# One projection stage of a hybrid decoder: the sample tile with its upper and lower parts side by side as one stationary operand

## What is computed

```python
def ab_project(x, pos, w_in):
    bn, n_len, _ = x.shape
    qa, ka, va, qb, kb, vb, gb = jnp.split(x @ w_in, 7, axis=-1)
    heads = lambda t: t.reshape(bn, n_len, -1, HEAD_DIM)
    return (rope(heads(qa), pos), rope(heads(ka), pos), heads(va),
            rope(heads(qb), pos), rope(heads(kb), pos), heads(vb), gb)
```

## Time and profile before

| | us |
|---|---|
| median of 3 runs | 2499.44 |
| lowest and highest | 2494.7, 2500.23 |
| span of the profiled execution | 2499.5 |
| PE busy | 2399.3 (96%) |
| DVE busy | 1621.7 (65%) |
| ACT busy | 1082.6 (43%) |
| all 28 pieces of PB1 and PB2, from first product to last | about 57 and 73 |

### The profile page before, as it was taken

One profiled execution on the slowest core, in us unless ns is written; L12 is line 12 of the kernel. 1 busy time (PEld: TensorE's weight loads), 2 busy tenths in 40 slices (PEclk: granted clock), 3 DMA queues, 4 the chain that ended last, 5 costly groups with the idle time before them and its releaser, 6 DMA issues.

```text
span 2499.5 us, 46319 instructions
## 1 busy us (share of the span) xinstructions
PE 2399.3 (96%) x18807; PEld 2262.1 (91%) x18807; DVE 1621.7 (65%) x2539; ACT 1082.6 (43%) x1657; POOL 468.4 (19%) x535
## 2 busy tenths in 40 slices
PE   7989999999899999999999999999999999999998
PEld 7988998999788777788999999999999898999997
DVE  5787776666775555577686566466656585587555
ACT  3433355433554333353353534455433637354332
POOL 4886810001200021300111101021001010121001
PEclk9999999999999999999999999999999999999998
DMA  8657766435446687644666556555554566555553
GB/s 181 172 161 206 206 186 202 127 110 152 118 143 200 194 281 219 176 121 110 172 175 174 164 152 198 182 154 155 152 152 144 174 196 204 151 168 144 153 151 105
DMA packets 676421, 417.84 MB, mean 167 GB/s; under 512 B 31570, under 2 KB 639698, under 8 KB 676210
## 3 DMA queue, kind: packets, MB, share of 16 engines
q1 hardware_dynamic: 669682, 394.51, 54.8%
q0 software_dynamic: 6528, 20.37, 2.6%
HBM read 396.04 MB, written 18.78 MB: 166 GB/s over the span
## 4 chain that ended last, share of the span: by engine, by line
PE 76%; DVE 13%; ACT 4%; issue 3%; SPq 2%; DMA 2%; POOL 1%; DVEq 0%; ACTq 0%; POOLq 0%
PE ps L270 21%; PE ps L272 20%; PE ps L271 20%; DVE w_lo L265 4%; PE ps L1004 2%; PE ps L1005 2%; PE ps L1006 2%; ACT w_hi L256 2%; PE ps L2403 1%; PE ps L1716 1%; PE ps L1765 1%; DMA w_raw<-in_ffn_w_up 1%; PE ps L1737 1%; DVE h_lo L467 1%; DVE x L557 1%
## 5 line engine op out<-in xcount | busy, mean ns | idle before, releaser
L265 DVE TENSOR_TENSOR w_lo<-w_raw,w_hi 128x1024 fp32r<-128x1024 f32 (+1 forms) x648 | 824.6, 1277 | 615.6 <-ACT w_hi L256 612.8
L270 PE MATMUL ps<-x_hi,w_hi 128*128 128x256 f32 (+1 forms) x3200 | 970.6, 303 | 33.6 <-DVE w_lo L265 23.7
L271 PE MATMUL ps<-x_lo,w_hi 128*128 128x256 f32 (+1 forms) x3200 | 955.3, 299 | 0.0
L272 PE MATMUL ps<-x_hi,w_lo 128*128 128x256 f32 (+1 forms) x3200 | 955.1, 298 | 0.0
L256 ACT ACTIVATE w_hi<-w_raw 128x1024 fp32r<-128x1024 f32 (+1 forms) x648 | 670.3, 1035 | 583.4 <-PE ps L272 419.6
L270 PEld LDWEIGHTS ps<-x_hi,w_hi 128*128 128x128 f32 x3200 | 615.5, 192 | 53.4 <-DVE w_lo L265 37.2
L271 PEld LDWEIGHTS ps<-x_lo,w_hi 128*128 128x128 f32 x3200 | 615.8, 192 | 1.1 <-issue 0.2
L272 PEld LDWEIGHTS ps<-x_hi,w_lo 128*128 128x128 f32 x3200 | 615.5, 192 | 0.0
L270 PE MATMUL ps<-h_hi,w_hi 128*128 128x256 f32 (+1 forms) x1408 | 422.5, 300 | 12.9 <-DVE w_lo L265 9.4
L271 PE MATMUL ps<-h_lo,w_hi 128*128 128x256 f32 (+1 forms) x1408 | 414.2, 294 | 0.0
L272 PE MATMUL ps<-h_hi,w_lo 128*128 128x256 f32 (+1 forms) x1408 | 414.2, 294 | 0.0
(11 more groups left out here) (281 smaller groups left out, 2184.5 us busy)
## 6 DMA issues: line engine op xcount, KB each, us to landing
w_raw<-in_ffn_w_gate SPq DMA_DIRECT2D x176, 512.0 KB, 4.1
w_raw<-in_ffn_w_up SPq DMA_DIRECT2D x176, 512.0 KB, 3.9
w_raw<-in_ffn_w_down SPq DMA_DIRECT2D x128, 512.0 KB, 4.0
w_raw<-in_w_in_ab SPq DMA_DIRECT2D x56, 512.0 KB, 4.1
w_raw<-in_ffn_w_down SPq DMA_DIRECT2D x64, 384.0 KB, 3.6
arena<-in_cache_k SPq DMA_DIRECT2D x64, 256.0 KB, 4.3
arena<-in_cache_v POOLq DMA_DIRECT2D x64, 256.0 KB, 4.7
w_raw<-in_w_out_ab SPq DMA_DIRECT2D x16, 512.0 KB, 4.0
```

The source lines that it names most:

```text
L265: dve.tensor_tensor(T.w_lo[:, u % RING, 0:n], T.w_raw[:, u % RAW, 0:n], T.w_hi[:, u % RING, 0:n].bitcast(F32), ALU.subtract).then_inc(T.w_ ...
L270: pe.matmul(out, w_hi, m_hi, start=first, stop=False)
L271: pe.matmul(out, w_hi, m_lo, start=False, stop=False)
L272: return pe.matmul(out, w_lo, m_hi, start=False, stop=last)
```

## The change

For the samples' tile alone, the 64 upper parts and the 64 lower parts are laid side by side as one stationary operand of 128 columns (`sample_tokens`, in the place of `h_hi`, which is free then). One product with `w_hi` gives hi·hi on partitions 0 to 63 and lo·hi on 64 to 127; a second, with the 64 upper columns alone and `w_lo`, adds hi·lo to partitions 0 to 63. So there are two products for each block instead of three. At the end of every section ACT moves partitions 0 to 63 to partitions 64 to 127 of a buffer in SBUF (`sample_rests`, in the place of `prod`), DVE adds that to the bank, and only then ACT empties it. At the start of PB1 and of PB2 ACT copies the samples' upper and lower parts into place, when PE has used all earlier pieces. The rotation of the samples' tile works on 64 partitions instead of 128.

Elsewhere, three counters (`h_rounded`, `rs_zeroed`, `zeroed`) become uses of the chain counter of DVE; at one place two memsets are then waited for one by one.

```diff
@@ class Project
+        self.rests = T.rests_moved.take(len(sections) if PT in self.tiles else 0)
+        self.copied = T.samples_copied.take(2 if PT in self.tiles else 0)
+        T.rests_added.close(len(sections) if PT in self.tiles else 0)
...
+def sample_tokens(T):
+
+    return T.h_hi.rearrange("p f n -> p (f n)")[:, 0:KT * P].rearrange("p (k n) -> p k n", k=KT)
+
+
+def sample_rests(T):
+
+
+    return T.prod[NS:P, :, :].rearrange("p a n -> p (a n)")[:, 0:MIX]
@@ project_tensor
+                if t == PT:
+                    if kk == 0:
+                        pe.wait_ge(T.samples_copied.h, R.copied + 2)
+                    both, own = sample_tokens(T)[:, kk], sample_tokens(T)[:, kk, 0:NS]
+                    if kk == 0:
+                        pe.matmul(out, both, w_hi, start=True, stop=False, skip_group_check=True)
+                        mm = pe.matmul(out[0:NS], own, w_lo, start=False, stop=False, skip_group_check=True)
+                    else:
+                        pe.matmul(out[0:NS], own, w_lo, start=False, stop=False, skip_group_check=True)
+                        mm = pe.matmul(out, both, w_hi, start=False, stop=(kk == KT - 1), skip_group_check=True)
+                    continue
                 pe.matmul(out, x_hi, w_hi, start=(kk == 0), stop=False)
                 pe.matmul(out, x_hi, w_lo, start=False, stop=False)
                 mm = pe.matmul(out, x_lo, w_hi, start=False, stop=(kk == KT - 1))
@@ project_scalar
-            act.activation(dst, T.ps[:, T.banks[R.o + n * j + i], 0:MIX], ACT.Silu if s == G_B else ACT.Copy)\
-               .then_inc(T.staged.h, 1)
+            out, r = T.ps[:, T.banks[R.o + n * j + i], 0:MIX], slice(NS if t == PT else 0, P)
+            if t == PT:
+                act.activation(sample_rests(T), out[0:NS], ACT.Copy).then_inc(T.rests_moved.h, 1)
+                act.wait_ge(T.rests_added.h, R.rests + j + 1)
+            act.activation(dst[r], out[r], ACT.Silu if s == G_B else ACT.Copy).then_inc(T.staged.h, 1)
...
     for sem, value in R.clear:
         act.wait_ge(sem.h, value)
+    if PT in R.tiles:
+        act.wait_ge(T.w_used.h, R.u)
+        if R.x_ready is not None:
+            act.wait_ge(T.x_ready.h, R.x_ready + KT)
+        for i, src in enumerate((T.x_hi, T.x_lo)):
+            act.activation(sample_tokens(T)[:, :, i * NS:(i + 1) * NS], src[:, :, SEQ:NT], ACT.Copy)\
+               .then_inc(T.samples_copied.h, 1)
@@ project_vector (rotate: every operand on partitions `at`, NS to P for the samples' tile)
+        at = slice(NS if t == PT else 0, P)
...
+        if q == 3 and PT in R.tiles:
+            out = T.ps[NS:P, T.banks[R.o + n * j + n - 1], 0:MIX]
+            dve.wait_ge(T.rests_moved.h, R.rests + j + 1)
+            dve.tensor_tensor(out, out, sample_rests(T), ALU.add).then_inc(T.rests_added.h, 1)
         yield
@@ S5Prepare, vector
-                    dve.memset(self.kernel[n][0:GH, :, 0:P], 0.0).then_inc(S.zeroed.h, 1)
-                dve.wait_ge(S.zeroed.h, 2)
+                    T.dve_chain(dve, dve.memset(self.kernel[n][0:GH, :, 0:P], 0.0))
```

More of the change, by code:

```diff
@@ L196, in open_trunk @@
     T.y_moved = [count("y_moved0"), count("y_moved1")]
-    T.tanh_done, T.silu_done, T.glu_done, T.h_rounded, T.h_done = map(
-        count, ("tanh_done", "silu_done", "glu_done", "h_rounded", "h_done"))
+    T.tanh_done, T.silu_done, T.glu_done, T.h_done = map(
+        count, ("tanh_done", "silu_done", "glu_done", "h_done"))
     T.res_done, T.acc_added, T.sum_done, T.centred = map(count, ("res_done", "acc_added", "sum_done", "centred"))
@@ L205, in open_trunk @@
     T.halves_added, T.scaled = count("halves_added"), count("scaled")
+    T.samples_copied, T.rests_moved, T.rests_added = map(count, ("samples_copied", "rests_moved", "rests_added"))
     T.dve_chain = Chain(ctx, nc, "dve_chain")
@@ L369, in __init__ @@
         self.u, self.o = len(T.pieces), len(T.banks)
-        self.tanh, self.silu, self.glu, self.rounded, self.h = (
-            c.take(n) for c in (T.tanh_done, T.silu_done, T.glu_done, T.h_rounded, T.h_done))
+        self.tanh, self.silu, self.glu, self.h = (
+            c.take(n) for c in (T.tanh_done, T.silu_done, T.glu_done, T.h_done))
         self.res_before = None if part == 0 else F.res
@@ L1057, in rotate @@
         t, r = R.tiles[i], n * R.nth[s] + i
+        at = slice(NS if t == PT else 0, P)
+        m = at.stop - at.start
         dve.wait_ge(T.staged.h, R.staged + n * j + i + 1)
[L1059 to L1063, removed]
+        heads = M.stage[at, i].rearrange("p (h j d) -> p h j d", h=HEADS, j=2)
+        sums = by_sin[at].rearrange("p (h j d) -> p h j d", h=HEADS, j=2)
+        dve.tensor_tensor(by_cos[at].rearrange("p (h d) -> p h d", d=HD // 2),
+                          M.stage[at, i].rearrange("p (h d) -> p h d", d=HD // 2),
+                          M.cos[at, t:t + 1, :].to_broadcast([m, HEADS * 2, HD // 2]), ALU.mult)
         for k in range(2):
             last = dve.tensor_tensor(sums[:, :, k], heads[:, :, 1 - k],
-                                     M.sin[:, t, k:k + 1, :].to_broadcast([P, HEADS, HD // 2]), ALU.mult)
+                                     M.sin[at, t, k:k + 1, :].to_broadcast([m, HEADS, HD // 2]), ALU.mult)
         T.dve_chain(dve, last)
-        dst = M.kb[R.g][:, i] if s == K_B else M.rot[:, i]
+        dst = M.kb[R.g][at, i] if s == K_B else M.rot[at, i]
         if s != K_B and R.turned + r >= n:
@@ L1072, in rotate @@
             dve.wait_ge(T.k_stored.h, M.k_stored[R.g])
-        last = dve.tensor_tensor(dst, by_cos, by_sin, ALU.add)
+        last = dve.tensor_tensor(dst, by_cos[at], by_sin[at], ALU.add)
         if s in (Q_B, K_B):
             T.dve_chain(dve, last)
-            d = (M.dq if s == Q_B else M.dk)[:, t, :].unsqueeze(2).to_broadcast([P, HEADS, HD])
+            d = (M.dq if s == Q_B else M.dk)[at, t, :].unsqueeze(2).to_broadcast([m, HEADS, HD])
             last = dve.tensor_tensor(dst.rearrange("p (h d) -> p h d", h=HEADS),
@@ L1546, in pick @@
                .then_inc(T.rs_picked.h, 1)
-        dve.memset(self.q_of[:, :, :, :], 0.0).then_inc(T.rs_zeroed.h, 1)
-        dve.wait_ge(T.rs_zeroed.h, 1)
+        T.dve_chain(dve, dve.memset(self.q_of[:, :, :, :], 0.0))
         for b in range(DEC_BATCH):
@@ L1994, in open_s5 @@
     S.made_taps = nc.dram_tensor("s5_made_taps", (KT, P, GT * P), F32, kind="Internal").ap()
-    S.sized, S.fallen, S.inverted, S.b_loaded, S.c_loaded, S.c_turned, S.c_placed, S.zeroed = map(
-        count, ("sized", "fallen", "inverted", "b_loaded", "c_loaded", "c_turned", "c_placed", "zeroed"))
+    S.sized, S.fallen, S.inverted, S.b_loaded, S.c_loaded, S.c_turned, S.c_placed = map(
+        count, ("sized", "fallen", "inverted", "b_loaded", "c_loaded", "c_turned", "c_placed"))
     S.formed, S.b_turned, S.b_moved, S.c_done, S.tapped, S.placed = map(
```

7 lines of the change are left out of this document (3 added, 4 removed).

## The result

The changed kernel takes 2511.31 us (2511.03 to 2511.73 over four runs) against 2499.14 before: a ratio of 1.005, 95% interval 1.0037 to 1.0063. It is slower, as forecast, by almost twice the forecast's 6.5 us, and 0.3 us above the range's upper end.

What follows compares the result with a forecast made beforehand. PE and DVE were taken as level in PB1 and PB2, so saved products become waits. Step-by-step delays of +2.3 us and clock drops of 4.4 gave +6.7 on 2499.44: 2506 us, range 2497 to 2511.

Steps and rivals of the forecast that it cites:

- What bounds the stages: In PB1 and PB2 PE and DVE are level; at four turns PE can come no earlier, however few its products.
- The rival in which PE's gain shows: Move and addition find engines free, nothing hangs on DVE, so 12.7 − 0.9 us goes: 2488 us; chance 0.08.
- Move and addition: At each section's end, 0.68 + 0.76 = 1.44 us between PE's last product and ACT's third emptying.
- step (c): In PB1, K_A's reciprocal waits for move and addition; the turn comes at 695.3 instead of 694.72, after waiting 3.4 us.
- The clock: Half-clock drops behind new waits of 3.4, 3.5 and 5.2 us in PB1 and PB2, 1.7 us each: together 4.4 us.
- step (a): At PB1's start the samples' first product waits for the copies, 1.3 us later; ACT's move comes at 662.1.
- the walk: Step-by-step timing without clock drops: PB1's third emptying 2.1 us later, PB2's end 0.15 later, +2.3 us in all.
- the rival without drops: The new waits in PB1 and PB2 leave the clock up, so only +2.3 us: 2501.8 us; chance 0.32.
- Drains: Changes between 64 and 128 columns drain PE, adding 1.6 us in PB1, 1.7 in PB2: 2509.5 with drops; chance 0.15.
- The change does what it says: Check against a rival that it does not: PE's list is 14934 rows instead of 14990, 56 fewer.
- What would show it: Turn waits of about 2, 3.4, 3.5, 5.2 us; K_A's reciprocal behind the addition; FFN's gate near 709 to 710.

Runs made afterwards that it cites:

- e2: The changed kernel without ACT's move and DVE's addition, the upper half of the samples' products left out of the result: 2498.61 us, ratio 0.9997.
- e10: The changed kernel with copies awaited one piece later, the addition one step later and writing the third emptying's output, unused products before four turns: 2495.47 us, ratio 0.9986.
- e5: The changed kernel with unused products into an unused bank, ahead of the waits at the four turns and before PB1's first samples' product: 2503.16 us, ratio 1.0013.
- e8: The changed kernel with DVE's addition one step later, writing straight to the third emptying's place except in G_B: 2499.25 us, ratio 0.9995.
- e12: The changed kernel itself, run again beside later experiments: 2511.70 us, ratio 1.005.
- e1: The changed kernel with unused products before each samples' turn, into the bank the turn will write, behind the wait for ACT: 2510.54 us, ratio 1.004.
- e3: The change in PB1 alone, PB2 multiplying as in the kernel before: 2505.47 us, ratio 1.0025.
- e6: The changed kernel with three products per part in the samples' first piece and the copies awaited one piece later: 2507.35 us, ratio 1.003.
- e7: The changed kernel with DVE's addition one step later, behind the norm's step that stood behind it: 2509.55 us, ratio 1.0037.

## Why the sign was right and the size was not

**What bounds the stages** was right. PE's saved products became waits at the turns, at all four; e2 shows that they are worth nothing that can be measured even when the sum is free, because of the waits and of the drops behind them. Only where fillings take those drops away, too (e10), do 3.1 us of the 12.7 show. The rival in which PE's gain shows is out for the change as made.

**Move and addition** were right in size. The timeline of ACT in the changed kernel, at the end of Q_A:

```profile
663.10 0.59 ACT L1054 ACTIVATE prod<-ps 64x512 f32<-64x512 f32 x1 [0.33 <-PE ps L1027]
664.47 0.60 ACT L1056 ACTIVATE arena<-ps 64x512 f32<-64x512 f32 x1 [0.78 <-DVE ps L1129]
```

And the timeline of DVE, the additions of Q_A and K_A, the reciprocal behind the second:

```profile
663.72 0.71 DVE L1129 TENSOR_TENSOR ps<-ps,prod 64x512 f32<-64x512 f32 x1 [1.90 <-ACT prod L1054]
...
683.83 0.71 DVE L1129 TENSOR_TENSOR ps<-ps,prod 64x512 f32<-64x512 f32 x1 [3.06 <-ACT prod L1054]
684.57 1.75 DVE L553 RECIPROCAL rstd<-rstd 128x256 f32<-128x256 f32 x1
```

Move to third emptying is 664.47 − 663.10 = 1.37 us (1.44 was taken), the addition 0.71 (0.69). The reciprocal stands behind the addition as step (c) said: K_A's move starts 5.9 us behind the first turn, and the turn follows the move by 15.1, where (c) had 4.2 and 15.0; the 1.7 us between 5.9 and 4.2 is, but for 0.1 to 0.2, the stretch at half clock from 677.7 to 681.0.

**The clock** is the step that failed, as the sum's term "together 4.4". It was worked out from three waits, those over 3.3 us, with one short drop at each. There were six behind this change in the trace, five of them at the copies and the turns, and three of those ran 5 us or more. The wait at the copies was in step (a) as 1.3 us of delay, which was right (the samples' first product is 6.82 from the start instead of 5.42), but not as a wait that lowers the clock; the first turn's 1.9 us was held too short for it, on the evidence of one wait of 2.50 without a drop, beside one of 2.20 with a drop. In numbers, at 47% of each stretch that lies on PE's products: PB1 6.1, 3.3 and 6.5 us (647.6 to 653.7, 677.7 to 681.0, 698.4 to 704.9) cost 2.9 + 1.5 + 3.1 = 7.5. With the walk's 2.1 that is 9.6; the third emptying is 66.21 − 56.75 = 9.5 later. PB2: 3.4 and 5.0 us cost 1.6 + 2.35, with 0.15 from the walk 4.1; measured 77.53 − 73.24 = 4.3. The drop behind the gate adds 1.5. So the two stages hold 2.3 of walk and 13 of clock, where the forecast had 2.3 and 4.4.

That the drops make this difference is shown by e5, which leaves move, addition and order as they are: 3.0 us above its own runs of the kernel before, where the rival without drops has 2.3, with the samples' first product held back by 1.6 us and one drop left behind the gate. The chain and the drops are not two causes side by side, though: the chain makes the waits and the drops follow the waits, so taking a link out of the chain (e8) brings back all 12 us, and taking the drops away (e5) some 9 of them. What the traces don't settle is the rest of the bookkeeping: 9.7 + 1.5 + 4.3 = 15.5 us in the stages and behind the gate against 12.2 in the medians. In the profiled executions the shared code gives back the difference, most of it between 800 and 920. There the kernel before waits 2.86 us ahead of a transpose at 804.55, with the clock at 0.50 behind it from 804.6 to 810.3; the changed kernel waits 1.76 us at that place, for cached keys to arrive, and stays at 1.00, which makes 3.6 of the 4.8 us. Most of the rest is a stretch of 5.9 us (852.4 to 858.3) for which the changed kernel's has one of 3.4 (858.5 to 861.9). This is no gain of the change: the same kernel, run again as e12, waits 3.13 us at the first place and has two stretches of about 3.4 us in this region.

**Drains**: none, as the pitch of 0.23 shows. **The change does what it says**: 56 products fewer.

**What would show it**: four waits, their sizes, the reciprocal's place and the shift at the gate's direction came as written; the gate came 714.78 instead of 709 to 710, 73.98 from the start instead of 66 to 67, by 7.5 us of drops.

## What to carry to other kernels

Where two engines are level at a hand-over, a saving on one of them becomes a wait, and a wait on TensorE can be paid twice: once as itself, if it moves the next hand-over, and again as products at half clock behind it. When a change lengthens TensorE's waits, count every new wait as a possible drop, also those that the walk calls harmless, price it at the long stretch of the trace rather than the short one, and see whether the link that makes the wait can go (here the addition writing where the emptying wrote, worth 12 us) before counting the products saved. Unused products in the wait are a cheap test of whether the clock is the cause; here they needed a bank of their own and a length under the wait (e1 had neither).

## What the hardware showed that was not expected

- **The same wait has either clock behind it.** 1.90 to 1.92 us at PB1's first turn: 0.50 behind it in the changed kernel, in e3 and in e12, 1.00 in e6 and e7. The kernel before has 1.00 behind 2.50 us of its wait at PB2's second turn; e3, with the same products there, has 0.51 behind it, windows of e3:

```profile
1086.70:1089.50 2.80, 0.02 (x1) 0.02 (x1) 2.70 (x6) 1.34 (x3) 0.00 (x0) 1.00 0.57 172
1091.30:1094.70 3.40, 3.40 (x9) 2.63 (x9) 3.40 (x6) 2.54 (x5) 0.00 (x0) 0.51 0.37 76
```

  One wait of one trace without a drop is no bound on what the clock does. The Trainium skill's TensorE: Matmul & The Clock Gate, section "HAM oscillation — how this bites in real kernels", tells of a kernel in which waits between short bursts of products put the array to half rate in each of its tiles, and of the gain there from keeping the products together. The five stretches of the changed kernel agree with the first, and the 8.2 us of e5 are what keeping it busy gave here.
- **Executions of the same code differ by up to 6 us at 640 us** (638.91 to 644.79), and the whole time of the kernel before by 11.4 us (2494.37 to 2505.76 over all runs of this study). How much of either is stretches at half clock is not shown.
- **64 columns cost as much as 128 and no more**: 0.23 us for 512 moving columns, also in between.
